# Expert retrieval in two table passes of 256 and 384 tokens, with the last 128 tokens' expert rows gathered

## The reference

```
expert = i1 * PEER_KEYS + i2                 # 128 (head, k) picks per token
g = jax.nn.softmax(best_s, axis=-1)
u = jnp.take(u_tab, expert, axis=0)          # rows of 1024 floats
act = gelu(einsum('thkd,td->thk', u, xc)) * g
vv = jnp.take(v_tab, expert, axis=0)
out = einsum('thk,thkd->td', act, vv)
```

## Time and profile before

| | |
|---|---|
| median of 3 runs (lowest to highest) | 3829.16 us (3824.23 to 3833.4) |
| the profiled execution: time, span of its instructions | 3836.49 us, 3834.8 us |
| mean granted clock of TensorE | 0.959 of full |
| busy: PE, PEld, DVE, ACT, POOL | 92%, 79%, 60%, 39%, 15% |
| HBM read and written | 591.09 MB, 67.11 MB |
| table tiles in / issued on SyncE's queue | 384 of 1024 KB |

### The profile page before, as it was taken

How to read it: one execution, slowest core, us unless ns; L and a number is a source line. 1 busy time by engine, 2 the same in 40 slices (tenths; PEclk the granted TensorE clock), 3 DMA queues, 4 the chain that set the end, 5 groups by cost and what they waited for, 6 DMA issues and landing times.

```text
span 3834.8 us, 59747 instructions
## 1 busy us (share of the span) xinstructions
PE 3530.4 (92%) x20722; PEld 3036.3 (79%) x20722; DVE 2289.9 (60%) x4186; ACT 1483.0 (39%) x2350; POOL 582.0 (15%) x292
## 2 busy tenths in 40 slices
PE   7889879998998679999999979999999999999998
PEld 7888767765644579998888869998888889999997
DVE  1233113654836888886666668886666665555555
ACT  1222223342102244444444444444444444444444
POOL 1321204321200024441000024441000000000000
PEclk9788989999999889999999989999999999999999
DMA  4443441111223356564554556564554565555654
GB/s 153 150 124 99 186 178 66 44 67 66 97 106 117 149 210 217 212 219 171 202 205 159 210 215 225 211 221 162 203 209 162 208 244 211 207 212 206 215 204 147
DMA packets 221239, 659.16 MB, mean 172 GB/s; under 512 B 12400, under 2 KB 159216, under 8 KB 163696
## 3 DMA queue, kind: packets, MB, share of 16 engines
q1 hardware_dynamic: 184960, 589.04, 42.4%
q10 hardware_dynamic: 35440, 67.11, 4.8%
q0 software_dynamic: 768, 2.10, 0.2%
HBM read 591.09 MB, written 67.11 MB: 172 GB/s over the span
## 4 chain that ended last, share of the span: by engine, by line
PE 69%; DVE 10%; issue 8%; ACT 6%; DMA 3%; DVEq 3%; ACTq 1%; POOL 0%; SPq 0%; POOLq 0%
PE ps L708 44%; PE ps L448 5%; PE ps L463 5%; DVE u_lo L1377 4%; PE ps L423 4%; ACT u_hi L1005 4%; PE ps L536 3%; PE ps L740 3%; DMA ring<-in_weights 1%; DVEq L1372 1%; ACTq L890 1%; PE ps L610 1%; DMA raw<-in_table 1%; PE ps L510 1%; PE ps L441 1%
## 5 line engine op out<-in xcount | busy, mean ns | idle before, releaser
L708 PE MATMUL ps<-h_hi,u_hi 128*128 128x256 f32 x3072 | 879.7, 286 | 10.5 <-DVE u_lo L1377 8.5
L708 PE MATMUL ps<-h_lo,u_hi 128*128 128x256 f32 x3072 | 870.0, 283 | 0.0
L708 PE MATMUL ps<-h_hi,u_lo 128*128 128x256 f32 x3072 | 869.3, 283 | 0.0
L708 PE MATMUL ps<-v_hi,c_hi 128*128 128x512 f32 x1536 | 618.6, 403 | 97.0 <-DVE c_lo L1397 97.0
L1377 DVE TENSOR_TENSOR u_lo<-raw,u_hi 128x1024 fp32r<-128x1024 f32 x384 | 472.4, 1230 | 366.7 <-ACT u_hi L1005 363.0
L708 PE MATMUL ps<-v_lo,c_hi 128*128 128x512 f32 x1536 | 606.8, 395 | 0.0
L708 PEld LDWEIGHTS ps<-h_hi,u_hi 128*128 128x128 f32 x3072 | 589.4, 192 | 21.5 <-issue 6.7
L708 PE MATMUL ps<-v_hi,c_lo 128*128 128x512 f32 x1536 | 604.5, 394 | 0.0
L708 PEld LDWEIGHTS ps<-h_lo,u_hi 128*128 128x128 f32 x3072 | 589.7, 192 | 9.9
L708 PEld LDWEIGHTS ps<-h_hi,u_lo 128*128 128x128 f32 x3072 | 589.3, 192 | 0.0
L1009 ACT CAST v_hi<-raw 128x1024 fp32r<-128x1024 f32 x384 | 402.9, 1049 | 239.8 <-PE ps L708 239.4
(11 more groups left out here) (160 smaller groups left out, 4835.8 us busy)
## 6 DMA issues: line engine op xcount, KB each, us to landing
raw<-in_table SPq DMA_DIRECT2D x384, 1024.0 KB, 4.8
ring<-in_weights SPq DMA_DIRECT2D x46, 2048.0 KB, 7.5
gate_in<-gate_scratch SPq DMA_DIRECT2D x192, 256.0 KB, 3.0
gate_scratch<-staged ACTq DMA_DIRECT2D x9, 4096.0 KB, 15.1
arena<-in_weights ACTq DMA_DIRECT2D x32, 512.0 KB, 6.8
gate_scratch<-staged ACTq DMA_DIRECT2D x3, 3840.0 KB, 12.5
arena<-in_x_t SPq DMA_DIRECT2D x2, 2048.0 KB, 11.9
score_scratch<-arena SPq DMA_DIRECT2D x8, 512.0 KB, 2.9
```

Source lines behind the costliest of these rows:

```text
L708: last = mm(out, a, b_, start=start and x == 0, stop=stop and x == len(pairs) - 1, skip_group_check=True)
```

## The change

The picks are now used in two ways. The first 640 tokens go through two table passes, of 256 tokens (pass 0, blocks 0 and 1) and 384 tokens (pass 1, blocks 2 to 4). The last block of 128 tokens (block 5) is gathered: for each of its 128 picks j, GpSimd issues an indirect DMA that fetches, for every token (partition), the 8 KB row (u and v) of its j-th expert. VectorE forms the dot product with the token (`row_dot`), ScalarE the Gelu and the gate, and VectorE adds the scaled v row to an accumulator (`row_add`). One pick is done per tile of pass 1, four row buffers (in the memory of `staged`) are in turn.

What moves with it:

- In pass 1 the score matmuls are 384 columns wide (24 of them), and `combine` has 18 matmuls instead of 12 and uses six banks.
- Only 160 gate steps are built instead of 192: 64 ahead of pass 0, and 96 in tiles 32 to 127 of pass 0 (three stages of 32 tiles, a block each). Pass 1 builds none.
- The 32 searches that are not in the trunk all run in pass 0: two in its first four tiles, then one in every four tiles up to tile 123, beside the gate steps.
- The gated one-hot is made by ScalarE, as four copies of 128 columns with a scale per partition (`scale_hot`); VectorE keeps the two one-hots.
- GpSimd no longer makes v_lo. VectorE makes all of it.
- `combine` runs two tiles behind `score` (LAG), and v_hi, v_lo are made for tile k-1 instead of k. u and v are loaded by separate DMAs of 512 KB.
- The trunk also stores block 5's h2 with tokens on partitions (8 transposes, a copy, a DMA of 512 KB). The host passes a second copy of the tables, by row.
- The end norms 256 tokens early in pass 1, and 512 (384 and the gathered 128) at its end.

The core of the diff:

```diff
+PHASES = ((0, 1), (2, 3, 4))
+GATHERED = 5
+WIDTH = tuple(P * len(b) for b in PHASES)
+LAG = 2
...
 @@ tensor
-                products(ps[:, t % 2, 0:TOK], pairs, True, True).then_inc(s_done, 1)
+                products(ps[:, t % 2, 0:WIDTH[n]], pairs, True, True).then_inc(s_done, 1)
...
-                for tb in range(2):
+                for tb in range(WIDTH[n] // P):
...
+            def body(n, i, building=None, first=False):
+                for t in range(4):
+                    k = 4 * i + (t + P * n)
+                    score(n, k, t)
+                    if not first or t >= LAG:
...
+                        combine(n, k - LAG, t, start=first and t == LAG)
+                    elif n:
+                        combine(n - 1, k - LAG, t, stop=t == LAG - 1)
+                    if building is not None:
+                        gate_step(4 * i + (FIRST_STEPS - P // 4 + t), t, building + 1)
 @@ scalar
+            def scale_hot(s, col, t):
+                act.wait_ge(hot2_ready, s + 1)
+                after(act, g_done, s - 1)
+                for x in range(4):
+                    last = A(hot2g[:, t % 2, x, :], hot2[:, t % 2, x, :], ACT.Copy, scale=sel_t[:, 2, bass.ds(col + x, 1)])
+                last.then_inc(hot2g_ready, 1)
+            def gathered(j, t):
+                act.wait_ge(dotted, j + 1)
+                after(act, row_used, j - 3)
+                A(dot[:, t:t + 1], dot[:, t:t + 1], ACT.Gelu)
+                act.drain()
+                A(cf[:, t:t + 1], dot[:, t:t + 1], ACT.Copy, scale=gate_g[:, bass.ds(j, 1)]).then_inc(cf_ready, 1)
 @@ scalar, body: gelu, u_hi(k+1), c_hi(k-1), scale_hot(s), copy_gates(s-1), v_hi(k-1), gathered
 @@ vector
+            def row_dot(i, t):
+                dve.wait_ge(row_in[t], 16 * i + 16)
+                V.tensor_tensor_reduce(out=rows[:, t, 0:D], in0=rows[:, t, 0:D], in1=x_tok, scale=1.0, scalar=0.0,
+                                       op0=ALU.mult, op1=ALU.add, accum_out=dot[:, t:t + 1]).then_inc(dotted, 1)
+            def row_add(j, t, opens=False):
...
+                dve.wait_ge(cf_ready, j + 1)
...
+                    stt(out=g_acc, in0=rows[:, t, D:2 * D], scalar=cf[:, t:t + 1], in1=g_acc,
+                        op0=ALU.mult, op1=ALU.add).then_inc(row_used, 1)
+            def body(n, i, stage=0, building=False, search_col=None, first=False, last=False, prep=None):
...
+                        coefficient(m, k - 1, 16 * i + (16 * (P // 4) * n + (16 if t else 0)), t + 3)
...
+                        hot_keys(4 * i + (FIRST_STEPS - P // 4 + t), 16 * i + (P * half - P * stage + 4 * t), t, stage + 1)
...
+                        split_u(k + 1, t + 1)
...
+                        split_coef(m, k - 1, t + 3)
+                        split_v(k - 1, t + 3)
+                    if n:
...
+                        row_dot(i, t)
+                        if not (first and t == 0):
+                            row_add(k - (P + 1), (t + 3) % 4, opens=first and t == 1)
...
+                    elif search_col is not None:
+                        search(False, i + 1, search_col, t)
 @@ gpsimd
-                        G.tensor_tensor(v_lo[:, t % 2, :], raw[:, t, D:2 * D], v_hi[:, t % 2, :].bitcast(F32),
-                                        ALU.subtract).then_inc(v_lo_ready, 1)
+            for j in range(P):
+                after(pool, row_used, j - 3)
+                G.indirect_dma_start(rows[:, j % 4, :], None, rows_in,
+                                     bass.IndirectOffsetOnAxis(ap=expert[:, j:j + 1], axis=0)
+                                     ).then_inc(row_in[j % 4], 16)
```

811 lines of the change are left out of this document (484 added, 327 removed).

## The result

The changed kernel takes 3421.70 us (median of 4 runs, 3413.95 to 3422.50) against 3828.51 us of four runs of the kernel before on the same chip: a ratio of 0.8933, 95% interval 0.8916 to 0.8949. The profiled execution spans 3420.8 us; the sum had said 3376.

The account below looks back on a forecast made before the run. It took TensorE, paced by matmul starts, as the bound in the last pass and a latency chain in gate tiles. Stretches summed to a span of 3376 us, 459 less than 3834.8, so 3829 - 459 = 3370 us, range 3290 to 3485.

Parts of the forecast that it names:

- The gates ahead of pass 0: 64 gate steps before pass 0: 1.3 us each instead of 2.07, 49 us gained, -44 with the split of h.
- The split of h: Ahead of the gate steps before pass 0: it waits for its load, charged at 5 us.
- The trunk: Before the gates: eight transposes, a copy and a store added beside full TensorE work, +1.5 us (0 to 4).
- Pass 0: 128 tiles of 256 columns: 901 us against 825; 96 gate tiles at 7.3 us, VectorE the bound by a little.
- The lag of two tiles takes the wait of combine off TensorE.: Pass 0 tiles: running combine two tiles behind removes its 0.70 us wait from TensorE; VectorE spends it again.
- The change of pass: Between pass 0 and pass 1: 24 us before, kept and rounded to 25 us (15 to 45).
- Pass 1: Tiles of 384 columns: 8.33 us each (8.27 to 8.44), 127 tiles 1058 us, with all row work hidden.
- The gather: Pass 1, GpSimd's indirect row load: 2 us each, bounds 0.56 to 5.4, hidden in the tile.
- TensorE paces pass 0: Rival: cheap scaled copies and overlapping waits make gate tiles 6.63 us, 64 us less, 3306 us; chance 0.13.
- The chain through ScalarE: Rival, pass 0: one-hot, scaled copies, gate step, its copy and v_hi in series, 8.2 us a tile, 3456 us; chance 0.09.
- VectorE paces pass 1: Rival: gathering slows VectorE by 1.44 us an operation; 10.5 us a tile, 3649 us, or 9.1, 3468; chance 0.10.
- The gather paces pass 1: Rival: a gather taking GpSimd or DMA queues 11.9 us erases the gain; 3970 us at 13 us; chance 0.05.

Follow-up runs that it names:

- the gates on VectorE: Changed kernel with the gated one-hot made by VectorE again everywhere, no scaled copies on ScalarE: 3443.59 us, ratio 0.8985.
- the gates shared: Changed kernel with GpSimd making pass 0's v_lo; ahead of pass 0 ScalarE makes three scaled copies, VectorE the fourth part fused: 3301.49 us, ratio 0.8611.
- v_hi is early: Changed kernel with ScalarE making v_hi before the four scaled copies and the gate copy in gate tiles: 3332.01 us, ratio 0.8696.
- no rows: Changed kernel with 127 of 128 gathers, their dot products, Gelus and scaled adds left out: 3410.25 us, ratio 0.8884.
- two more dots: Changed kernel with each gathered row's dot product made three times from the fifth tile of pass 1 on: 3418.85 us, ratio 0.8920.
- twice the rows: Changed kernel with rows fetched a second time, from the fifth pick on, into a buffer nothing reads: 3438.69 us, ratio 0.8970.
- GpSimd's v_lo: Changed kernel with GpSimd instead of VectorE making v_lo in all of pass 0: 3316.87 us, ratio 0.8644.

## Why the prediction was right, and where it was off

The direction and most of the size were right; the forecast was 52 us low, of which the ledger has 45 in the span: +26.7 ahead of pass 0, +34.2 in pass 0, -11.5 after it, -4.5 in the tail. Luck is in it twice. The sum started from 1403.9 us for the first c_hi, where the trace has 1399.3, so the gain forecast ahead of pass 0 was too large by 31 us and not 27. And in pass 0 two errors cancel in part.

- **The gates ahead of pass 0** (-44 us, bounds to nothing). The 64 steps were mis-sized: 1.68 us each and not 1.3, and they gained 23 us and not 49. The term was the scaled copy, 0.19 us by a line through two casts and 0.30 in the rows, because the line had no scale per partition in it; L877 in the kernel before had shown its 0.10 us. With the gates on VectorE a step is 2.08 us, with the gates shared 1.48: taking work off ScalarE moves the step, as a full engine would have it.
- **The split of h** (5 us). The first one-hot starts 16.1 us later than before, of which 6.3 are in the trunk and 9.7 in the stretch with the split; 4.6 us are saved between the last gate copy and the first c_hi, where the split stood before. So this cost 5.2, as forecast.
- **The trunk** (+1.5 us). The token vectors of the last group are stored at 1166.50 us instead of 1160.46, before most of the added work, at a granted clock of 0.80 against 0.82 in the first 300 us. In the other runs the first c_hi moves by as much either way. So these 6.3 us can't be laid to the change.
- **Pass 0** (901 us, measured 935.2). The early tiles are 5.75 us, as forecast, and the first 32 take 194.7 for 193. The gate tiles are the term that was mis-sized: 7.85 for 7.3, which over 96 tiles is 52 us. Against that, the 18 us that the sum had for the split of the next h, the three borders and the short softmax operations hardly show: the 7.85 is a mean with two borders in it. From tile 32 on it had 708 us, and they were 740.4. VectorE's sum of 6.84 was near (6.96 once v_hi is early). The standing before v_lo was put at 0.35 us (3.35 against 3.05 is 0.30) and is 0.80; the path was named rightly, through the scaled copies to v_hi, but with copies that were 0.42 us too short in all. VectorE also pauses where its loop of four tiles turns, 0.63 us, and in all 0.23 us a tile before the coefficient. No engine is named for it, and with v_hi early it is there as well (19.3 us in 86 tiles).
- **"The lag of two tiles takes the wait of combine off TensorE."** Right in sign; it is worth 20 us in the median, at the stage borders and the change of pass, and not 0.70 us a tile. The row of 0.70 us in the earlier trace rows names "issue" and not c_lo. The waits of TensorE in the kernel before, from 1600 to 2200 us, do name c_lo, with 0.4 us a tile:

```profile
PE ps L708 <- DVE c_lo L1397: 33.5, 60, 1.9
```

- **The change of pass** (25 us): 14.6, and 2 more in the next eight tiles. The wait for the token vectors, 10 us, is there; the change is still shorter than forecast.
- **Pass 1** (8.33 us a tile): 8.307. The width of 384 columns starts matmuls (8.307 - 18 x 0.230)/24 = 0.1736 us apart, 0.001 from the midpoint. VectorE's work is 566.26/800 x 8.307 = 5.9 us (6.2), the dot product 1.14 and the add 1.20 by starts, no second pass through the data. 277 GB/s for 275, a share of 0.78. All of it hidden, as the kernels with no rows, with two more dots and with twice the rows showed for the steady tiles; what does not hide are the 12.8 us of the first rows.
- **The gather** (2 us of GpSimd, 0.56 to 5.4): 1.02. The fit in the Trainium skill, "DMA: Bandwidth & Descriptors", section "Anatomy of one DMA — SWDGE (gpsimd) path", gave an estimate of 4.4 us a gather; the trace has 5.7 us from issue to landing beside the table stream, and hides it three tiles deep. The row of the gathers in the changed kernel, from 2500 to 3300 us:

```profile
DMA to landing us min/median/max: 5.5/5.7/6.1
```

- **The tail** (31 us): 26.5.

Of the rivals, "TensorE paces pass 0" is not this kernel but the one with GpSimd's v_lo, at 3317 for the 3306 priced, and there it took an edit and not cheap copies. "The chain through ScalarE" stood at 8.2 us a tile; the truth, 7.85, lies between it and the forecast. "VectorE paces pass 1" falls: a gather stretched no wide operation (means of 1219 to 1285 ns in pass 1, against 1222 to 1280 before), where by the widest reading of the rule that the prediction quotes from the Trainium skill all six could have been met. "The gather paces pass 1" needed 11.9 us of GpSimd or of the queues for one gather; GpSimd takes 1.02, and two gathers a tile left the tile at 8.307.

What stays open: the pause of 0.63 us, the 0.12 us left over in the shared steps, the two late loads when rows are fetched twice, and the scatter of the first c_hi by up to 22 us between executions.
